# Three of eight expert visits multiply the raw fp32 weights in two 64-column tiles

## The reference, cut to what matters

```python
def swiglu(h, wg, wu, wd):
    return (jax.nn.silu(h @ wg) * (h @ wu)) @ wd

logits = (hf @ w_router).astype(jnp.float32)      # hf: 256 x 1024
topv, topi = lax.top_k(logits, TOP_K)             # the best 2 of 8 experts
wts = jax.nn.softmax(topv, axis=-1)
gate = jnp.sum(jax.nn.one_hot(topi, N_EXPERTS) * wts[..., None], axis=1)
for e in range(N_EXPERTS):                        # wg, wu: 1024 x 3584, wd: 3584 x 1024
    out = out + gate[:, e:e + 1] * swiglu(hf, wg[e], wu[e], wd[e])
```

## Time and profile before

| what | value |
|---|---|
| median of the runs | 1713.88 us |
| span of the profiled execution | 1710.3 us |
| the runs' median less that span | 3.6 us, which lie outside the span |
| TensorE busy | 1647.6 us (96%) |
| VectorE busy | 1262.1 us (74%) |
| ScalarE busy | 1054.6 us (62%) |
| data read from HBM | 475.61 MB |

### The profile page before, as it was taken

The page is one execution under the profiler, slowest core; times in us unless marked ns, Lnnn a source line. Parts: engine busy times, 40 slices in busy tenths (PEclk is TensorE's granted clock), DMA queues, the critical chain, the costliest instruction groups (busy, mean ns, idle before and its releaser), DMA issues. The chain is left out here.

```text
span 1710.3 us, 22950 instructions
## 1 busy us (share of the span) xinstructions
PE 1647.6 (96%) x9429; PEld 1429.8 (84%) x9429; DVE 1262.1 (74%) x928; ACT 1054.6 (62%) x885; POOL 48.1 (3%) x113
## 2 busy tenths in 40 slices
PE   8999999999999999899988999998999988999997
PEld 8999899989999989788866788776888767888886
DVE  4555645455556565678899898898989898988986
ACT  5443555344454445367688777787777787777774
POOL 1000000000000010150000000000000000000000
PEclk9999999999999999999999999999999999999999
DMA  9555535465655554689999999899999899998970
GB/s 328 175 195 173 203 123 173 153 205 172 196 187 184 186 172 160 249 313 350 378 356 396 354 369 363 343 397 389 366 355 381 346 395 364 366 363 338 379 262 25
DMA packets 164104, 478.08 MB, mean 280 GB/s; under 512 B 8516, under 2 KB 13732, under 8 KB 164004
## 3 DMA queue, kind: packets, MB, share of 16 engines
q1 hardware_dynamic: 164004, 476.69, 76.1%
HBM read 475.61 MB, written 1.05 MB: 279 GB/s over the span
## 5 line engine op out<-in xcount | busy, mean ns | idle before, releaser
L553 ACT ACTIVATE whi<-raw 128x2048 fp32r<-128x2048 f32 (+1 forms) x260 | 490.7, 1896 | 251.2 <-PE ps L1355 108.3
L921 DVE TENSOR_TENSOR wlo<-raw_more,whi 128x2048 fp32r<-128x2048 f32 x192 | 437.5, 2290 | 63.9 <-ACT whi L553 63.5
L916 DVE TENSOR_TENSOR wlo<-raw,whi 128x2048 fp32r<-128x2048 f32 (+1 forms) x116 | 259.0, 2236 | 211.2 <-ACT whi L553 211.1
L553 ACT ACTIVATE whi<-raw_more 128x2048 fp32r<-128x2048 f32 x192 | 366.5, 1915 | 60.5 <-PE ps L1708 28.5
L921 DVE TENSOR_TENSOR wlo<-raw,whi 128x2048 fp32r<-128x2048 f32 x144 | 325.3, 2288 | 41.8 <-ACT whi L553 41.6
L1679 PE MATMUL ps<-whi,a_hi 128*128 128x512 f32 x1120 | 349.3, 393 | 0.0
L1355 PE MATMUL ps<-a_hi,whi 128*128 128x256 f32 x992 | 281.4, 284 | 0.0
L1355 PE MATMUL ps<-a_hi,wlo 128*128 128x256 f32 x992 | 280.7, 283 | 0.0
L1355 PE MATMUL ps<-a_lo,whi 128*128 128x256 f32 x992 | 280.7, 283 | 0.0
L1679 PEld LDWEIGHTS ps<-whi,a_hi 128*128 128x128 f32 x1120 | 207.3, 188 | 43.9 <-DVE wlo L921 2.3
L1679 PE MATMUL ps<-wlo,a_hi 128*128 128x512 f32 x560 | 218.7, 391 | 0.0
(11 more groups left out here) (252 smaller groups left out, 2147.0 us busy)
## 6 DMA issues: line engine op xcount, KB each, us to landing
raw_more<-in_w_e_up SPq DMA_DIRECT2D x80, 1024.0 KB, 7.3
raw_more<-in_w_e_gate SPq DMA_DIRECT2D x64, 1024.0 KB, 6.6
raw<-in_w_e_down SPq DMA_DIRECT2D x64, 1024.0 KB, 7.0
raw<-in_w_e_gate SPq DMA_DIRECT2D x48, 1024.0 KB, 7.6
raw_more<-in_w_e_down SPq DMA_DIRECT2D x48, 1024.0 KB, 7.6
raw<-in_w_in SPq DMA_DIRECT2D x32, 1024.0 KB, 5.4
raw<-in_w_e_up SPq DMA_DIRECT2D x32, 1024.0 KB, 7.3
raw<-in_w_xk SPq DMA_DIRECT2D x8, 1024.0 KB, 5.7
```

What stands on the lines that cost most here:

```text
L553: return act.activation(dst, src, ACT.Copy, scale=scale)
L916: dve.tensor_tensor(wlo[n % SPL][:, 0:size], raw[n % RAW][:, 0:size], whi[n % SPL][:, 0:size].bitcast(F32), ALU.subtract).then_inc(s["lo_r ...
L921: return dve.tensor_tensor(dst, src, hi.bitcast(F32), ALU.subtract)
```

## The change

Light visits no longer split their weights. TensorE reads the unit's buffer directly, as plain fp32. The gathered tokens of a light visit are one fp32 tile `he_slots64` of 64 slots. The tensor engine's array is used as two tiles of 128 rows by 64 columns: the matmuls of a block's first half write the output partitions 0 to 63 (tile position column 0) and those of the second half write partitions 64 to 127 (column 64), of the same bank.

In a unit of 4 blocks there are then 4 matmuls of 64 stationary columns by 512 moving columns. Their order is by tile: the two k blocks of the first half, then the two k blocks of the second. The gate and up units of the last group are 8 matmuls of 256 columns, four k blocks of one half and then four of the other. A light visit thus has 38 x 4 matmuls of 512 columns and 4 x 8 of 256, and the three light visits together have 552.

Other parts that go with it:
- Both halves of the hidden activations of a whole group lie in one tile of 128 partitions by 512, so one transposition of 128 by 128 serves both (14 transpositions for each light visit, 28 for a heavy one), and `light_fold` and the second split are gone.
- ScalarE and VectorE do for a light visit only what stands in the new `light_visit`: three or four short instructions for each group. The 42 splits are gone.
- SP waits for `unit_used` instead of `lo_ready` where a buffer was last used by a light visit.
- The output of a light visit lies in one bank as two halves, and its scatter uses 64 rows of the array.
- ScalarE may split the first three units of a heavy visit while the light one before it still runs (`enter`).
- Visit 6 is written out instead of being the loop's first pass (`STEADY` 7), and waits are counted by new helpers (`every`, `split_only`, `split_units`, `steps`).

```diff
-STEADY = 6
+STEADY = 7
...
-    fold2 = place("fold_halves", [P, HP], F32, g0)
-    st = place("silu_half", [P, 4, HP], F32, g0 + 256)
-    at_ = place("act_half", [P, 4, HP], F32, g0 + 1280)
+    he64 = place("he_slots64", [P, KD, HP], F32, place_of["a_hi"] + 4096)
+    aT64 = [place(f"actT_pair{i}", [P, 4, P], F32, place_of["mem_lo"] + 2048 * i) for i in range(2)]
...
-        LIGHT_T_AFTER = {**T_AFTER, NJ - 1: DOWN[-1] - 3}
+        LIGHT_T_AFTER = [GATE[g + 1] + 1 for g in range(len(GROUPS) - 1)] + [DOWN[-1] - 2]
...
                 def slot_wait(i, v):
-                    if i != DOWN[0]:
-                        n = i + 1 if i == DOWN[0] - 1 else i
-                        sp.wait_ge(s["lo_ready"], v * BODY + (U0 + n - MR + 1))
+                    pv, pi = (v, i - MR) if i >= MR else (v - 1, i + BODY - MR)
+                    if isinstance(pv, int) and pv in LIGHT:
+                        sp.wait_ge(s["unit_used"], pv * BODY + U0 + pi + 1)
+                    else:
+                        sp.wait_ge(s["lo_ready"], split_units(pv, pi + 1))
...
+                def gathered64(v):
+                    for b in range(2):
+                        act.wait_ge(s["g_done"], every(v, 2, b + 1))
+                        copy(he64[:, 4 * b:4 * b + 4, :],
+                             bank(3 * b).rearrange("p (k c) -> p k c", c=P)[:, :, 0:HP]).then_inc(s["hehi_ready"], 1)
...
+                def enter(v):
+                    if isinstance(v, int) and v in LIGHT:
+                        gathered64(v)
+                    else:
+                        expert_hi(0, v)
+                        gathered_hi(v)
+                        for i in range(1, AHEAD):
+                            expert_hi(i, v)
+                def silu64(g, v):
+                    w = GROUPS[g][1] * C // 2
+                    act.wait_ge(s["unit_used"], every(v, BODY, U0 + GATE[g] + 2 * GROUPS[g][1]))
+                    if g >= 2:
+                        act.wait_ge(s["act_ready"], steps(v, g - 1))
+                    else:
+                        act.wait_ge(s["t_done"], steps(v, 0))
+                    act.activation(silu_t[g % 2][:, 0:w], bank(g % 2)[:, 0:w], ACT.Silu).then_inc(s["silu_ready"], 1)
+                def actT64(g, v):
+                    n = 2 * GROUPS[g][1]
+                    act.wait_ge(s["t_done"], steps(v, g + 1))
+                    copy(aT64[g % 2][:, 0:n, :], bank(6).rearrange("p (f c) -> p f c", c=P)[:, 0:n, :]
+                         ).then_inc(s["actT_ready"], 1)
                 def light_visit(v):
-                    for i in range(AHEAD, BODY):
-                        expert_hi(i, v)
-                        if i == AHEAD:
-                            y_hi(v)
-                        for g, (j, n) in enumerate(GROUPS):
-                            if i == GATE[g] + 2 * n + 1:
-                                act.wait_ge(s["unit_used"], v * BODY + (U0 + GATE[g] + 2 * n))
-                                if g == 0:
-                                    act.wait_ge(s["act_ready"], v * NJ)
-                                else:
-                                    act.wait_ge(s["t_done"], v * NJ + j)
-                                for c in range(n):
-                                    copy(silu_t[c][:], bank(c)).then_inc(s["gs_ready"], 1)
-                            if i == UP[g] + 2 * n + 1:
-                                act.wait_ge(s["unit_used"], v * BODY + (U0 + UP[g] + 2 * n))
-                                act.wait_ge(s["t_done"], v * NJ + j)
-                                for c in range(n):
-                                    copy(act_t[c][:], bank(2 + c)).then_inc(s["us_ready"], 1)
-                        for j in range(NJ):
-                            if i == LIGHT_T_AFTER[j] + 2:
-                                act.wait_ge(s["t_done"], v * NJ + (j + 1))
-                                act.activation(st[:], bank(6)[:, 0:4 * HP].rearrange("p (f c) -> p f c", c=HP), ACT.Silu
-                                               ).then_inc(s["silu_ready"], 1)
-                            if i == LIGHT_T_AFTER[j] + 3:
-                                act.wait_ge(s["act_ready"], v * NJ + (j + 1))
-                                copy(aTh[j % 2][:, :, 0:HP], at_[:]).then_inc(s["acthi_ready"], 1)
-                    next_visit(v, P)
+                    y_hi(v)
+                    silu64(0, v)
+                    for g in range(1, len(GROUPS)):
+                        if g < len(GROUPS) - 1:
+                            actT64(g - 1, v)
+                            silu64(g, v)
+                        else:
+                            silu64(g, v)
+                            actT64(g - 1, v)
+                    actT64(len(GROUPS) - 1, v)
...
+                def act64(g, v):
+                    w = GROUPS[g][1] * C // 2
+                    dve.wait_ge(s["unit_used"], every(v, BODY, U0 + UP[g] + 2 * GROUPS[g][1]))
+                    dve.wait_ge(s["silu_ready"], steps(v, g + 1))
+                    dve.wait_ge(s["t_done"], steps(v, max(g - 1, 0)))
+                    dve.tensor_tensor(act_t[g % 2][:, 0:w], silu_t[g % 2][:, 0:w], bank(2 + g % 2)[:, 0:w], ALU.mult
+                                      ).then_inc(s["act_ready"], 1)
...
+                    y_lo(v)
+                    add_piece(0, v)
+                    add_piece(1, v)
+                    act64(0, v)
+                    add_piece(2, v)
+                    add_piece(3, v)
+                    act64(1, v)
+                    st_and_select(v)
+                    for g in range(2, len(GROUPS)):
+                        act64(g, v)
...
                 def light_gate_up(i, v):
+                    w_name, g, part = order[i]
+                    n_c = GROUPS[g][1]
+                    kk = 4 // n_c
+                    o = bank((0 if w_name == "gate" else 2) + g % 2)
+                    if part == 0 and g >= 2:
+                        pe.wait_ge(s["act_ready"], steps(v, g - 1))
+                    unit_landed(i, v)
+                    w = moe_raw(i).rearrange("p (k n) -> p k n", k=kk)
+                    n = n_c * C // 2
+                    if i in (0, 2):
+                        pe.wait_ge(s["hehi_ready"], every(v, 2, i // 2 + 1))
+                    for c in range(2):
+                        for k in range(kk):
+                            kt = kk * part + k
+                            ins = pe.matmul(o[c * HP:(c + 1) * HP, 0:n], he64[:, kt, :], w[:, k, c * n:(c + 1) * n],
+                                            start=kt == 0, stop=kt == KD - 1)
+                    ins.then_inc(s["unit_used"], 1)
...
+                def light_t(g, v):
+                    pe.wait_ge(s["act_ready"], steps(v, g + 1))
+                    if g == 0:
+                        pe.wait_ge(s["xadd_done"], every(v, 4, 1))
+                    else:
+                        pe.wait_ge(s["actT_ready"], steps(v, g))
+                    for f in range(2 * GROUPS[g][1]):
+                        ins = pe.transpose(bank(6)[:, f * P:(f + 1) * P], act_t[g % 2][:, f * P:(f + 1) * P], ident[:])
+                    ins.then_inc(s["t_done"], 1)
+                def light_down(i, v):
+                    _, g, part = order[i]
+                    n = 2 * GROUPS[g][1]
+                    pe.wait_ge(s["actT_ready"], steps(v, g + 1))
+                    unit_landed(i, v)
+                    w = moe_raw(i).rearrange("p (k n) -> p k n", k=2)
+                    for c in range(2):
+                        for k in range(2):
+                            f = 2 * part + k
+                            half = f // n
+                            ins = pe.matmul(bank(4)[c * HP:(c + 1) * HP, :],
+                                            aT64[g % 2][:, f % n, half * HP:(half + 1) * HP], w[:, k, c * C:(c + 1) * C],
+                                            start=g == 0 and f == 0, stop=g == len(GROUPS) - 1 and f == 2 * n - 1)
+                    ins.then_inc(s["unit_used"], 1)
...
-                        ins = pe.matmul(bank(6 if n == 0 else 7), ST[:, t * P:(t + 1) * P], y[:, c * C:(c + 1) * C],
-                                        start=m == 0, stop=m == 1)
+                        if isinstance(v, int) and v - 1 in LIGHT:
+                            slots = slice(c * HP, (c + 1) * HP)
+                            lhs, rhs = ST[slots, t * P:(t + 1) * P], y[slots, 0:C]
+                        else:
+                            lhs, rhs = ST[:, t * P:(t + 1) * P], y[:, c * C:(c + 1) * C]
+                        ins = pe.matmul(bank(6 if n == 0 else 7), lhs, rhs, start=m == 0, stop=m == 1)
```

More of the change, by code:

```diff
@@ L55, in trunk @@
     BODY = 6 * NJ
+    HEAVY = NE - len(LIGHT)
     WINDOWS = (2, 4, 8, 16)
@@ L304, in trunk, with lights, every, split_only @@
                 T_AFTER[j + c] = GATE[g + 1] + 2 * c if g + 1 < len(GROUPS) else DOWN[g] - 1
-        LIGHT_T_AFTER = {**T_AFTER, NJ - 1: DOWN[-1] - 3}
```

(53 more changed lines are left out.)

206 lines of the change are left out of this document (79 added, 127 removed).

## The result

The changed kernel takes 1642.74 us (1642.42 to 1643.05, 2 runs) against 1713.88 us before. The ratio is 0.9587, 95% interval 0.9572 to 0.9603: 71 us, 4.1% faster. I had forecast 1720 us, with a range from 1703 to 1830 us, and had left out of it the one rival that ended on this side, full overlap at 1619 us.

The account below looks back on a forecast made before the run. TensorE was taken to bound heavy visits, a split-buffer loop light ones. A light visit was 110.4 + 6.9 + 1.5 = 118.8 us against 116.5, three times +6.9 us in all, giving about 1720 us, range 1703 to 1830.

Parts of the forecast that it names:

- full overlap: Light visits' two column tiles: each has its own queue, so order by tile costs nothing; 1619 us, chance 0.20.
- The bound before: Expert visits: heavy ones bound by TensorE (122.4 us), light ones by a loop through three split buffers (116.5 us).
- the rest of a visit: Gather, scatter, transpositions and selection: 8.1 us in a heavy visit, 6.9 us in a light one.
- The price of a record: Plain fp32 on TensorE: two records per matmul, a step of 0.431 us per 512-column record.
- side by side, but started in program order: Light units: a record finding its tile busy blocks those behind; six steps for eight records, 110.4 us a visit.
- theory A: Experiments' theory on light units: each tile has its own queue, so tile B's record starts while earlier A records wait.
- rival 2: Light visits: each tile change shows its weight load, at most 0.19 us for 84 changes; 1769 us, chance 0.08.
- Rival 1: Light visits: the two tiles do not overlap at all; 153.2 us a visit, 1824 us in all, chance 0.27.
- Rival 3: Light visits: tiles overlap fully, TensorE needs 80.8 us and the DMA binds instead; 1619 us, chance 0.20.
- the ring's lead: Weight loads: 14 buffers of lead carry the first light visit, leaving 3.7 units; each heavy visit wins 6.
- changes of shape: TensorE switching between whole-array and two-tile matmuls, 18 times a light visit: 0 to 2.9 us, taken as 1.5.
- Costs put at nothing: Short VectorE and ScalarE work, later buffer release, early splits and heavy visits (staying 122.4 us) were priced at zero.

Follow-up runs that it names:

- e10: Kernel before the change, with light visits loading a quarter of each unit's bytes: 1714.0 us, ratio 1.0001 to the kernel before.
- e2: Changed kernel with both halves' products on the same 64-column tile: 1834.05 us, ratio 1.0705 to the kernel before.
- e4: Changed kernel with light visits loading quarter bytes and four units taken together, 16 records of one tile before 16 of the other: 1760.19 us.
- e6: Changed kernel with light visits loading quarter bytes and two units taken together, runs of 8 records on a tile: 1677.97 us.
- e11: Changed kernel with quarter loads, four units taken together and light visits' operands read as bf16: 1485.36 us in one run.
- e1: Changed kernel with the two tiles' matmuls of a light unit alternating instead of ordered by tile: 1643.05 us, ratio 0.9594 to the kernel before.
- e3: Changed kernel with light visits loading a quarter of each unit's bytes, products unchanged: 1626.18 us, ratio 0.9489 to the kernel before.

## Why the prediction was wrong

**The bound before** was right. e10 shows that the light visits were not bound by the DMA, and the 122.4 us of a heavy visit were read rightly. What I put into them was not. The period from 963.26 to 1085.62 us does not hold 504 matmuls of a heavy visit: it holds 40 heavy units of 12 and the last two units of the light visit at 8. These 496 matmuls take 112.6 us, so the rest of a visit is 9.8 us and not 8.1, and each light visit of the forecast was 1.7 us too short by it.

**The price of a record** was right: 0.431 us by columns for the whole array, 0.429 us measured on a 64-column tile (e2).

**The step that failed** is "side by side, but started in program order. A record that finds its tile busy then holds up all behind it." I took it because the rows of before show starts in the order of the program. But on one array a queue in order and a queue for each tile look the same, so those rows could not decide it, and I gave them weight that they did not have. What the runs show in its place: a record whose tile is free starts while up to three records of the other tile wait ahead of it, and only a fourth waiting one holds it up (A's fifth of 8 and thirteenth of 16 start with B's first). Whether each tile has its own places, as theory A says, or both share one look-ahead of four waiting records is open: the orders tried here give the same starts either way. A unit of the change has runs of just four, so nearly all of it is paired: four steps for a unit's eight records where my sum had six, and 86.9 us for the first light visit where it had 118.8. Had its runs been 16, I would have been nearer: e4 is slower than before.

The Trainium skill's rule that matmuls start and end strictly in program order ("TensorE: Matmul & The Clock Gate", Part 3) is what I had put beside this. The traces of e4, e6 and e11 go against it for starts, so the measurement decides. The Trainium skill's other rule in that part, that weight loads overlap with matmuls in flight only where the row group differs, I had read as making each change of tile dear; in the changed kernel the loads of 0.137 us lie under the other tile's matmuls and show nowhere in the step, so rival 2 falls too. One line, L1665, least, median and greatest duration in ns:

```profile
L1665 PEld LDWEIGHTS ps<-raw,he_slots x288: 132/137/138, 854.7 to 1351.4; 128*64 128x64 f32 x144
L1665 PE MATMUL ps<-raw,he_slots x288: 378/592/643, 854.7 to 1351.6; 128*64 128x512 f32 x96, 128*64 128x256 f32 x48
```

The "up to 2 times" of the Trainium skill's page "TensorEngine Tiling (Array Packing)", section "Theoretical Speedup", held for runs of four: eight records in four steps of 0.429 us. At 16 to a run it was out of reach (e4).

**Rival 1**'s 153.2 us for the visit was luck in part. The period of e2 holds two units of the heavy visit before in place of two light ones, about 1.4 us less than the sum had (24 steps of 0.227 us for 16 of 0.429), and the rest of a visit is 1.7 us more.

**Rival 3** had the mechanism, both halves of it: full overlap (without the limit that e4 and e6 show), and then the DMA with the ring's lead. Its 1619 us was 24 us short, and the periods say where:
- A light visit takes 86.9 us where the DMA doesn't bind, not 80.8. Of the 6.1 us, some 2.2 are only the cut: the period from gather to gather holds two units of the heavy visit before. The misread rest of a visit is 1.7, and 1.5 are the 256-column units, which have runs of eight and so start with four records alone (e1 takes them away). What is left, under 1 us, would be changes of shape beyond the 1.5 us assumed; no run takes it apart.
- The three light visits take 265.8 us, not 255.
- The heavy visits between them take 382.7 us, not the 367.2 that I kept for them. 12.3 us of that came with the DMA. A heavy visit must have its first unit loaded and split before TensorE can use it, and my count let the lead run down to nothing at no cost; nor did it hold the fall of the granted clock behind each long hole. 1.1 us each are changes of shape (123.5 in e3 against 122.4).

**Costs put at nothing**: ScalarE's and VectorE's short work in light visits costs nothing that shows: TensorE is busy for all 86.8 us of visit 1. The later release of buffers does not hold up TensorE there either. Whether it cost lead for later is not shown: from 855 to 865 us, with SP waiting for TensorE, the DMA moved 245 GB/s, but it also fell, to 183, at the same place before. The heavy visits were not free, as said.

**The range** failed because it had room for only one side. Two rivals on the slow side were more alike than I treated them: both rest on tiles that hinder each other, for which no row spoke.

## What to carry to other kernels

Products on two 64-column tiles run side by side at full rate each, so 64 tokens in plain fp32 cost about what two fp32r products on the whole array cost (1.72 us a unit against 8 steps of 0.227, 1.82 us), and the split work on ScalarE and VectorE is saved. The order matters only through the length of a run on one tile: up to four records, which is two plain fp32 matmuls, is free; at eight each stretch pays four records at its start and end; at 16 the gain is gone. When such a change makes one stage faster than the loads, look at which stage refills the ring, and place the fast ones behind it. A wait of TensorE for a load can cost more than its length: look at the granted clock just behind it.

## What the runs showed of the hardware that was not expected

- A tile's first record started 6 ns after the record of the other tile that stood four from the end of its run (A's thirteenth of 16 and fifth of 8 in plain fp32, fifth of 8 in bf16).
- How it is with more than two tiles, and with row tiles, was not tried, nor an order that tells places for each tile from one look-ahead for both.
- After a hole of 3.2 us ahead of heavy visits 4 and 6 TensorE's granted clock was 0.50; it stayed at 1.00 behind the 1.40 us hole of visit 2.
- From a whole-array matmul to a two-tile one the step is 0.32 us (854.39 to 854.71), against 0.227 within the former: about 0.09 us for a change of shape.
- The DMA held 403 to 409 GB/s for some 650 us of 1 MiB loads (slices 22 to 37 of the page).
